# Partition maximum by transpose and ones product, value pages one tile later, weight remainders on VectorE

## The reference

```python
z = x @ w_in                     # q, k, v, u and two gates; 2048 -> 8192
# prompt: differential attention over 256 keys
# sample b: the same over 2048 past keys (16 pages of 128) and the new one
s = einsum(q, k) * HEAD_DIM ** -0.5 + bias
p = softmax(s)                   # two maps per head, 8 heads: 16 maps
attn = einsum(p[:, :, 0] - lam * p[:, :, 1], v)
ssm = s5_branch(u, ...)          # complex diagonal recurrence, GELU, GLU
merged = gate_a * (attn @ w_proj_attn) + gate_s * (ssm @ w_proj_ssm)
h = layer_norm(alpha * x + merged @ w_out)
y = layer_norm(alpha * h + conv_ffn(h))   # up 2048 -> 11008, conv of width 3, down 5504 -> 2048
```

## Time and profile before

| | us |
|---|---|
| median of 3 runs | 1958.56 (1956.56 to 1960.93) |
| the profiled execution, its time | 1960.97 |
| its span | 1959.1 |
| TensorE busy | 1791.6 (91%) |
| VectorE busy | 1110.0 (57%) |
| ScalarE busy | 604.7 (31%) |
| POOL busy | 1116.0 (57%) |

### The profile page before, as it was taken

The page is one execution under the profiler, slowest core; times in us unless marked ns, Lnnn a source line. Parts: engine busy times, 40 slices in busy tenths (PEclk is TensorE's granted clock), DMA queues, the critical chain, the costliest instruction groups (busy, mean ns, idle before and its releaser), DMA issues.

```text
span 1959.1 us, 32040 instructions
## 1 busy us (share of the span) xinstructions
PE 1791.6 (91%) x11898; PEld 1530.8 (78%) x11898; DVE 1110.0 (57%) x1360; ACT 604.7 (31%) x927; POOL 1116.0 (57%) x383
## 2 busy tenths in 40 slices
PE   7899998898988969967999799999999997999997
PEld 5787665565655636646999799999999997999995
DVE  1353656556565563345950389999999999000004
ACT  2021222232222320212322354444444443333333
POOL 1036455465554643004777457777777777677771
PEclk9999898898988978978999989999999999999997
DMA  9766897888989866655656436666666665666651
GB/s 213 180 202 221 282 337 246 297 298 272 322 275 310 288 213 231 196 173 136 180 164 173 129 100 181 174 173 173 172 173 172 173 173 141 171 174 176 175 149 45
DMA packets 537197, 393.44 MB, mean 201 GB/s; under 512 B 23618, under 2 KB 502743, under 8 KB 536535
## 3 DMA queue, kind: packets, MB, share of 16 engines
q1 hardware_dynamic: 404944, 325.07, 55.4%
q10 hardware_dynamic: 132160, 67.11, 12.3%
HBM read 385.47 MB, written 7.02 MB: 200 GB/s over the span
## 4 chain that ended last, share of the span: by engine, by line
PE 55%; issue 14%; DMA 9%; DVE 9%; POOL 8%; SPq 3%; ACT 3%; DVEq 0%; ACTq 0%; POOLq 0%
PE bank L966 12%; PE bank L972 12%; PE bank L967 12%; PE bank L670 11%; DMA work<-in_cache_k 7%; POOL work L583 4%; POOL weights_lo L620 3%; PE bank L638 2%; DMA weight_ring<-in_w_in 2%; ACT weights_hi L1339 1%; PE bank L658 1%; DVE work L1615 1%; SPq L460 1%; SPq L398 1%; PE bank L751 1%
## 5 line engine op out<-in xcount | busy, mean ns | idle before, releaser
L620 POOL TENSOR_TENSOR weights_lo<-weight_ring,weights_hi 128x2048 fp32r<-128x2048 f32 (+1 forms) x166 | 750.5, 4532 | 371.6 <-ACT weights_hi L1339 208.8
L670 PE MATMUL bank<-work,weight_ring 128*128 128x264 f32 x2176 | 555.7, 411 | 7.8 <-DMA weight_ring<-in_w_in 7.3
L670 PEld LDWEIGHTS bank<-work,weight_ring 128*128 128x128 f32 x2176 | 425.1, 201 | 130.8 <-issue 56.7
L583 POOL TENSOR_TENSOR work<-work 128x1024 f32<-128x1024 f32 x128 | 299.2, 2352 | 212.0 <-DMA work<-in_cache_k 139.6
L1339 ACT ACTIVATE weights_hi<-weight_ring 128x2048 fp32r<-128x2048 f32 (+1 forms) x166 | 309.3, 1863 | 332.8 <-PE bank L967 315.6
L966 PE MATMUL bank<-h_hi,weights_hi 128*128 128x264 f32 x1376 | 345.1, 289 | 8.0 <-DVE h_lo L1811 8.0
L967 PE MATMUL bank<-h_lo,weights_hi 128*128 128x264 f32 x1376 | 340.7, 286 | 0.0
L966 PEld LDWEIGHTS bank<-h_hi,weights_hi 128*128 128x128 f32 x1376 | 260.7, 189 | 11.4 <-issue 8.4
L967 PEld LDWEIGHTS bank<-h_lo,weights_hi 128*128 128x128 f32 x1376 | 261.1, 190 | 0.0
L1615 DVE TENSOR_REDUCE work<-work 128x16 f32<-128x1024 f32 x128 | 153.9, 1216 | 165.8 <-POOL work L583 165.5
L972 PE MATMUL bank<-h_hi,weights_lo 128*128 128x264 f32 x1376 | 183.7, 286 | 5.6 <-POOL weights_lo L620 5.6
(11 more groups left out here) (233 smaller groups left out, 2192.0 us busy)
## 6 DMA issues: line engine op xcount, KB each, us to landing
weight_ring<-in_w_up SPq DMA_DIRECT2D x86, 1024.0 KB, 5.6
work<-in_cache_k SPq DMA_DIRECT2D x128, 512.0 KB, 6.0
work<-in_cache_v SPq DMA_DIRECT2D x128, 512.0 KB, 6.6
weight_ring<-in_w_in ACTq DMA_DIRECT2D x60, 1024.0 KB, 12.1
weight_ring<-in_w_down SPq DMA_DIRECT2D x32, 1024.0 KB, 5.9
weight_ring<-in_w_out SPq DMA_DIRECT2D x16, 1024.0 KB, 5.9
weight_ring<-in_w_down SPq DMA_DIRECT2D x16, 704.0 KB, 4.7
weight_ring<-in_w_proj_attn SPq DMA_DIRECT2D x16, 512.0 KB, 4.0
```

The source lines that it names most:

```text
L583: pool.tensor_tensor(page(k_pages, n), page(k_pages, n), q_b[b % 2], ALU.mult).then_inc(kq_ready, 1)
L620: pool.tensor_tensor(w_lo[:, cols].bitcast(F32R), slot3(off % SLOTS, 0, k_tiles).rearrange("p k m -> p (k m)"), w_hi[:, cols], ALU.subtrac ...
L670: last = pe.matmul(bank[n % 2][:, 0:N], slot(n % SLOTS, k), tiles[k], start=(k == 0), stop=(k == len(tiles) - 1))
```

## The change

Three things are edited.

1. `global_max` on POOL goes. TensorE transposes the 128 x 16 maxima into 16 x 128 (`max_rows`, in the middle of a weight tile), VectorE takes the maximum of each row and multiplies it into a 16 x 16 diagonal (`all_max`), TensorE multiplies ones by the diagonal, so that all partitions have all 16 maxima in bank 2 (`global_max`), and the shift reads them there, placed inside `states(t, 1)`. Both products are entries of `MAIL_ORDER`.
2. The value pages of sample i start in tile g(4i) instead of u(i+2); pages 11 to 15 fall into the next turn. The scores get a third buffer. SP's interleaving, ScalarE's order, and the place of `combine` and `denominators` follow.
3. `low` moves from POOL to VectorE, one tile ahead of its use, in front of the work on each tile.

```diff
-    MAIL_ORDER += [("combine", _i - 1)] if _i else []
+    MAIL_ORDER += [("max_rows", _i), ("max", _i)] + ([("combine", _i - 1)] if _i else [])
@@ SP
-            load_values(0, 0)
+            for p in range(4):
+                load_values(0, p)
...
-                for p in range(1, 4):
-                    load_values(i, p)
-                for keys, values in (((4, 5), (4, 5)), ((6,), (6,)), ((7, 8), (7, 8, 9)), ((9, 10), (10,)),
-                                     ((11,), (11, 12, 13)), ((12, 13), (14,)), ((14, 15), ())):
+                if i:
+                    load_values(i - 1, 15)
+                    load_values(i, 0)
+                    load_values(i, 1)
+                for keys, values in (((4, 5), (2, 3, 4, 5)), ((6, 7, 8), (6, 7, 8, 9, 10)), ((9, 10, 11), (11, 12, 13)),
+                                     ((12, 13, 14, 15), (14,))):
...
@@ POOL
-            def global_max(b):
-                pool.wait_ge(smax_ready, b + 1)
-                wait(pool, ssub_ready, b)
-                pool.partition_all_reduce(small[:, 528:544], small[:, 512:528], P,
-                                          bass.bass_isa.ReduceOp.max).then_inc(gmax_ready, 1)
...
@@ PE
+            def max_rows(b):
+                post(("max_rows", b))
+                pe.wait_ge(smax_ready, b + 1)
+                transpose(bank[2][0:16, 0:P], small[:, 512:528]).then_inc(mail, 1)
+
+            def global_max(b):
+                post(("max", b))
+                pe.wait_ge(gmax_ready, b + 1)
+                pe.matmul(bank[2][:, 0:16], ones[0:16, :], small[0:16, 528:544], start=True, stop=True).then_inc(mail, 1)
...
+                if whole:
+                    z_tile(("v", i + 1), before(11, 12, 13))
+                    scores(i, 1, 1)
+                    z_tile(("u", i + 2), before(14, 15), lambda: max_rows(i))
                 else:
-                    z_tile(("v", i + 1))
-                scores(i, 1, 1)
-                if i + 2 < HT:
-                    z_tile(("u", i + 2), i, (0, 1))
+                    z_tile(("v", i + 1), before(11, 12, 13, 14), lambda: max_rows(i))
+                    scores(i, 1, 1)
+                global_max(i)
+                cx(t, 0)
+                bu(t, 2)
+                scores(i, 0, 0)
+                z_tile(("g", 4 * i), now(0, 1, 2) if whole else before(15))
+                scores(i, 0, 1)
                 if i:
                     combine(i - 1)
                 denominators(i)
...
@@ DVE
+            def all_max(b):
+                dve.wait_ge(mail, MAIL["max_rows", b] + 1)
+                wait(dve, mail, MAIL["max", b - 1] + 1 if b else 0)
+                dve.tensor_reduce(small[0:16, 544:545], bank[2][0:16, 0:P], AX.X, ALU.max).then_inc(mail_read, 1)
+                dve.wait_ge(mail_read, MAIL["max_rows", b] + 1)
+                dve.tensor_scalar(small[0:16, 528:544], ident[0:16, 0:16], small[0:16, 544:545], None, ALU.mult
+                                  ).then_inc(gmax_ready, 1)
...
                 page_max(i)
                 states(t, 0)
-                shift(i)
                 reduce_pages(b, 0, 1)
-                states(t, 1)
+                all_max(i)
+                states(t, 1, lambda: shift(i))
+                maxima(i, 1)
                 page_sums(i)
-                maxima(i, 1)
...
+            def low(m, off, k_tiles=KT):
+                dve.wait_ge(wh_ready, m + 1)
+                dve.wait_ge(slot_done, PROJ0 + m - 1)
...
+                    low(n + 1, j + 1)
```

More of the change, by code:

```diff
@@ L200, in build @@
         cut = cutter(work, 21760, 23936)
-        score = [cut(288) for _ in range(2)]
+        score = [cut(288) for _ in range(2)] + [work[:, 12384:12672]]
         s_sb, ax0, sums, w_new = cut(768), cut(512), cut(256), cut(64)
@@ L613, in _ @@
                     products(i + 1, p)
[L614 to L626, removed]
-                low(SPLIT_DOWN - SPLIT_DOWN % 4 + j, j, KT)
-            with pool.Fori(0, KT // 4) as i:
-                for o in range(12):
-                    k0, k1 = DOWN_PARTS[o % 3]
-                    low(12 * i + SPLIT_DOWN + o, SPLIT_DOWN + o, k1 - k0)
         @block.tensor
@@ L798, in denominators @@
                 pe.wait_ge(lsum_ready, b + 1)
-                pe.matmul(bank[2][:, 0:32], ones[:, :], score[b % 2][:, 256:288], start=True, stop=True).then_inc(mail, 1)
+                pe.matmul(bank[2][:, 0:32], ones[:, :], score[b % 3][:, 256:288], start=True, stop=True).then_inc(mail, 1)
             def combine(b):
@@ L864, in _, with before, now @@
             for i in range(H - 1):
-                t = i + 1
+                t, whole = i + 1, i + 2 < HT
+                def before(*pages):
+                    return [(i - 1, p) for p in pages if i]
+                def now(*pages):
+                    return [(i, p) for p in pages]
                 bu(t, 0)
@@ L1547, in _, with states @@
             bias3 = bias.rearrange("p (h x) -> p h x", h=H)
-            def states(t, p):
+            def states(t, p, between=None):
                 n = 4 * t + p
@@ L1714, in _ @@
             dve.tensor_tensor(gelu_t, gelu_t, yg, ALU.mult).then_inc(gelu_dve, 1)
+            all_max(B - 1)
+            shift(B - 1)
+            maxima(H - 1, 1)
             page_sums(B - 1)
-            maxima(H - 1, 1)
             dve.wait_ge(gelu_act, 2)
@@ L1776, in merge @@
                                       ALU.subtract).then_inc(merged_ready, 1)
+            low(0, 0)
             merge(0)
@@ L1852, in _, with down @@
             up(FT // 2, 1)
-            with dve.Fori(0, KT // 4) as n:
-                ch.enter(n, 0, 4)
+            def down(n, last=False):
                 for j in range(4):
                     tile = bass.ds(4 * n * N + j * N, N)
+                    for o in range(3 * j + 1, 3 * j + 4):
+                        if not (last and o == 12):
+                            k0, k1 = DOWN_PARTS[o % 3]
+                            low(12 * n + SPLIT_DOWN + o, SPLIT_DOWN + o, k1 - k0)
                     dve.wait_ge(slot_done, 12 * n + UP + 3 * j + 3)
@@ L1860, in _ @@
                                              ).then_inc(zv_read, 1)
-            ch.leave(KT // 4)
+            with dve.Fori(0, KT // 4 - 1) as n:
+                ch.enter(n, 0, 4)
+                down(n)
+            ch.leave(KT // 4 - 1)
+            down(KT // 4 - 1, True)
             norm(1)
```

124 lines of the change are left out of this document (64 added, 60 removed).

## The result

The changed kernel takes 2001.2 us (median of 4 runs, 1998.13 to 2006.92); the kernel before took 1959.26 beside it. The ratio is 1.0225, with a 95% interval of 1.0201 to 1.0249: slower by 42 us. The forecast was 1990.

The account below looks back on a forecast made before the run. Neither TensorE nor DMA was full; a chain through a key page, the all-reduce and VectorE bound it. Terms 36.5-3+11+9.5+1-23.8 = +31.2 on 1961.0 gave 1992, as a median 1990 us; range 1932 to 2012.

Parts of the forecast that it names:

- The order of the keys on SP: SP's queue in a turn: key pages move behind later value pages, so TensorE waits 6 us for the differences.
- G to X: First part of a turn, gate tile g0's start until the last key pages go out: 50.7 us, where 34.8 stood.
- X to M: Second part of a turn, last key pages' issue to the per-partition maximum's end: 20.5 us, where 22.0 stood.
- M to G: Third part of a turn, per-partition maximum's end to the next g0: 17.0 us instead of 25.0.
- Six turns, +36.5: Attention stage, first g0 to last: six turns of 88 us, 528 us against 491.5.
- Last turn and g28: End of attention: differences later in the turn without tile u, +11; waits for and behind the maximum in g28, +9.5.
- The wait for V9: GLU tiles: TensorE's 20.92 us wait for this value page some 5 shorter but beginning 6 later, +1.
- Remainders, -23.8: Product stages: weight remainders on VectorE instead of POOL shorten TensorE's waits, -23.8 us, give or take 4.
- The maximum, 8 us a turn: Attention turn: POOL's all-reduce, 8.57 us of the chain, goes for TensorE products and small VectorE instructions; 8 less a turn.
- Turns as long as before: Rival, attention: VectorE reaches the differences in time, turns stay 81 to 83 us; 1938 us, chance 0.18.
- Transfers bound the turn: Rival, attention: the transfer hole during the all-reduce is filled, turns 75 us with slack; 1883 us, chance 0.10.
- VectorE was not too full: Rival, late in the kernel: VectorE's remainder subtraction takes POOL's 4.53 us, +21 on the forecast, 2011 us; chance 0.06.

Follow-up runs that it names:

- k9_ahead: The changed kernel with only the last seven key pages issued earlier on SP's queue: 1930.6 us, ratio 0.9869 to the kernel before.
- keys_ahead: The changed kernel with the sixth to eighth and the last seven key pages all issued earlier on SP's queue: 1896.6 us, ratio 0.9703 to the kernel before.
- allreduce_back: The changed kernel with the maximum over the partitions back on POOL as one all-reduce, without the two TensorE products: 2061.1 us, ratio 1.0511 to the kernel before.
- k6_ahead: The changed kernel with only the sixth to eighth key pages issued earlier, ahead of V4, on SP's queue: 1943.5 us, ratio 0.9932 to the kernel before.
- maxima_early: params_pool with VectorE's score maxima of block 1 behind states(t,0) instead of behind states(t,1): 1849.2 us, ratio 0.9442 to the kernel before.
- params_pool: keys_ahead with the seven loads of conv and LayerNorm parameters on POOL's queue instead of SP's: 1878.4 us, ratio 0.9597 to the kernel before.
- the last two: maxima_early, and the same kernel with V9 issued between K'13 and K'14 instead of behind K'15: 1849.2 and 1822.8 us.

## Why the prediction held, point by point

The sum was +31.2 us on the span, and +38.7 were measured. By the rows of the table, measured less forecast is -0.9, +13.0, +9.6, -8.6, -0.8 and -4.8: errors of 23 us one way and 15 the other, so the sum is nearer than its terms.

**The order of the keys on SP: right, and shown.** The late K'6 was to cost 6 us a turn; it cost 5.80 in the turn shown and 6.4 in the mean of six (53.8 less 15.3, by 6). K'12 behind V13: k9_ahead.

**G to X, 50.7: right.** From 495.90 to the end of V9's product, 547.18, are 51.3. X to M, 20.5: the maximum ends at 567.60, 20.4 behind. M to G, 17.0: 583.70 less 567.60 is 16.1. The turn shown is 87.8 us, forecast 88, but it is the shortest of the six. The maximum on VectorE:

```profile
566.99 0.61 DVE L1628 TENSOR_REDUCE small<-work 128x16 f32<-128x272 f32 x1
```

**Six turns, +36.5: too small by 13.** The mean turn is 90.2. By the prediction's own cuts, in the mean of the six turns, G to X is 52.8 us for 50.7 forecast, X to M 21.2 for 20.5, and M to G 16.1 for 17.0. The mis-sized term is G to X, and in it the low clock behind the wait ahead of G: from the start of g0 to the end of g1 I had 23.8 us with 2 for the clock, and measured were 25.3. Three of the six stretches take 26.5 to 26.7 us at a granted clock of 0.84 to 0.85, the others 23.2 to 24.5 at 0.92 to 0.93. The wait for the differences is 6.4 for 6, what is behind it 21.1 for 20.9.

I also counted two waits a turn, and there are three: the transposed maxima stand in the middle of tile u, and TensorE waits there for the per-partition maximum, 2.2 to 3.2 us in five turns and 14.2 in the sixth, which has no tile u. This wait is not in the sum and need not be, since the sum runs over VectorE from M on: M to G is 16.1 to 16.3 us in all six turns, behind the 14.2 as behind the 2.2.

**Last turn and g28: 20.5 forecast, 21.5 measured, by luck: the terms are others.** The wait for the differences is 15.35 us at 807.11, 10.5 over the earlier trace rows (forecast 10). Ahead of g28 comes a stretch that I did not see, the samples' part of cx: 3.38 us of waiting for VectorE and 32 products in 6.42 us instead of 3.66, +6.8 in all from g3's end to g28. In g28 itself the 9.5 us did not come: the maximum was ready, and only 1.02 was waited for what follows.

```profile
807.11 0.88 PE L615 MATMUL bank<-ident,work 128*128 128x128 f32 x3 [15.35 <-DVE work L1603]
...
843.88 6.42 PE L848 MATMUL bank<-work 128*128 128x32 f32 x32 [3.38 <-DVE work L1707]
...
865.22 0.36 PE L783 MATMUL bank<-small,ones 16*128 16x16 f32 x2 [1.02 <-DVE small L1636]
...
924.56 1.05 PE L635 MATMUL bank<-work 128*16 128x256 f32 x8 [19.91 <-DMA work<-in_cache_v]
```

**The wait for V9: half right.** I had it some 5 us shorter and beginning 6 later. It is 1.0 shorter (19.91 for 20.92), and V9's product starts 50.8 us behind the first GLU tile instead of 42.1; in return it has one tile fewer behind it. With the remainders' part the stretch is -6.8, forecast -6.

**Remainders, -23.8: right alone, -23.5.** TensorE's wait ahead of the projections went from 11.88 to 3.45 us (forecast 5), the one ahead of the down products from 9.2 to 1.8 (forecast 1.9), the fifteen for remainders from 5.6 to 0.8. One remainder takes 2.22 us on VectorE, where the earlier trace rows has 4.53 on POOL:

```profile
L1778 DVE TENSOR_TENSOR weights_lo<-weight_ring,weights_hi 128x2048 fp32r<-128x2048 f32 (+1 forms) x166 | 369.0, 2224 | 119.1 <-ACT weights_hi L1341 64.1
```

The product stages gained 4.8 us more than forecast. The three waits inside them that went or shrank (9.2, 5.6 and 2.4 before) account for 14.6 of the 21.6; the other 7 are busy time (1013.4 to 1006.2 us for the same 7990 products), at a granted clock of 0.98 for 0.97. I had put 1.5 on the clock.

**The maximum, 8 us a turn: right in its number, wrong in its reason.** The step said that the all-reduce "holds 8.57 us of the chain and goes". The shift comes no earlier; the prediction's own list already had 8.6 us of VectorE's work and a part of states(t,1) ahead of it. What is 9 us shorter is the way from the shift to g0: 14.0 us before (542.66 to 556.69), 4.6 after (491.33 to 495.90). The first value pages, the combination and the sums no longer stand in it. And the all-reduce, put back into the new order, costs 53 to 60 us, with POOL out for 16.6 to 18.0 us in the turns read and other waits on TensorE than the one predicted. The Trainium skill (GPSIMD Engine Reference, section 4.1) would have the reduction along the partitions on GPSIMD. The runs disagree in the new order of the turn (1.0511 against 1.0225); in the old order the kernel with the all-reduce is as fast as the new one without (0.9694 against 0.9703), and no run has the products with ones there.

**The rivals.** Turns as long as before fell, by the 5.80 us. "Transfers bound the turn" fell for the change as it was made, but its condition, the last keys early enough, is what k9_ahead and keys_ahead set up; its 73 to 75 us a turn were reached and passed at 68.1. VectorE was not too full: 2.22 us each, and no wait for it over 1 us in the projections.

**The signs.** The shifts are 87.8 to 92.6 us apart, where 86 to 91 was named; two of six are over. The wait for the differences is 4.9 to 8.9 us in the six turns (named: 4 to 8). K'12 was issued behind V9's product, DMA traffic was low behind g1 (0.39 from 528 to 541), the longest single VectorE instruction behind the start of the projections took 2.3 us, and the wait ahead of the down products is 1.8. All of these were named.

## What to carry to other kernels

When products are moved later, look at what shares a queue with the loads that their buffers hold back: here every key page behind a value page moved with it, and one line of SP's order was worth 105 us, where the whole change cost 42. What an instruction costs depends on what is queued behind it on its engine: the same all-reduce cost 53 to 60 us in one order of the turn, and in another the kernel that has it is as fast as the one that doesn't. Its share of the chain, 8.57 us, told neither. And when a wait is taken away, ask which queue it was hiding: twice here the next one was longer.

## What was not expected of the hardware

- A partition all-reduce of 128x16 has a record of 0.39 us, and POOL's profile shows nothing else for 16.4 us before the change (533.43 to 549.83) and for 18.0 in allreduce_back: about 8 us ahead of the record and 7 to 10 behind. The profile calls both "issue"; what POOL does in them it doesn't show. Before the change:

```profile
531.07 2.36 POOL L583 TENSOR_TENSOR work<-work 128x1024 f32<-128x1024 f32 x1 [0.43 <-DMA work<-in_cache_k]
542.24 0.39 POOL L588 PARTITION_ALL_REDUCE small<-small  x1 [8.81 <-issue]
549.83 4.65 POOL L583 TENSOR_TENSOR work<-work 128x1024 f32<-128x1024 f32 x2 [7.20 <-issue]
```

- One DMA of 129 KB (conv_w, in rows of 128 elements) held SP's queue for 21.3 us; the loads of the LayerNorm parameters behind it hold it for 0.4 to 0.9 each.
- A wait cost TensorE more than itself in these runs: 47 us of waits taken away in k6_ahead gave 58, 14.4 in maxima_early gave 29, the rest being busy time of the same products (10.0 and 17.8 us less). The granted clock, as the mean over a kernel, rose from 0.935 (the changed kernel) over 0.956 (keys_ahead) and 0.957 (params_pool) to 0.969 and 0.975 with the last two.
